# Latent mixer: order of the state factors, the first two heads' scores, the pooling products and the pooled splits

## The reference, cut to what matters

```python
h_lat, h_ctx = mlstm_bidir(p[..., :M_COLS], pc[..., :M_COLS], conv_w[l], conv_b[l], w_q[l], w_k[l], i_bias[l], f_bias[l])
mix = jnp.concatenate([mlstm_out(h_lat, p[..., 2 * M_W:3 * M_W], head_norm[l]),
                       pool_mixer(p[..., M_COLS:], pool_w[l], pool_scale[l], True)], axis=-1)
x = ada_out(x, mix @ w_out[l], mod, 1, norm_post[l, 1], 1.0)
```

## Time and profile before

| | us |
|---|---|
| median of 3 executions | 2033.75 |
| lowest, highest | 2031.55, 2034.03 |
| the profiled execution, its own time | 2034.56 |
| its span, first to last instruction | 2032.7 |
| TensorE busy (matmul) | 1994.2 |
| VectorE busy | 1351.2 |
| ScalarE busy | 1104.4 |
| mean granted TensorE clock | 0.997 |

### The profile page before, as it was taken

One profiled execution on the slowest core, in us unless ns is written; L12 is line 12 of the kernel. 1 busy time (PEld: TensorE's weight loads), 2 busy tenths in 40 slices (PEclk: granted clock), 3 DMA queues, 4 the chain that ended last, 5 costly groups with the idle time before them and its releaser, 6 DMA issues.

```text
span 2032.7 us, 27622 instructions
## 1 busy us (share of the span) xinstructions
PE 1994.2 (98%) x10892; PEld 1687.8 (83%) x10892; DVE 1351.2 (66%) x2199; ACT 1104.4 (54%) x1722; POOL 74.1 (4%) x151
## 2 busy tenths in 40 slices
PE   7999999999989999999999999999999999999998
PEld 5988899987768888888897788888888897788887
DVE  4457676666777556655598897655665587987652
ACT  4344466445565446554646766545654646666552
POOL 0000000001010000000100000000000100000000
PEclk9999999999999999999999999999999999999999
DMA  9797755674257746655533466555755534457551
GB/s 340 250 305 257 236 189 178 208 266 156 99 187 246 229 157 217 205 180 206 198 125 127 145 227 218 184 170 160 239 179 197 204 120 149 142 190 235 186 184 45
DMA packets 281906, 392.91 MB, mean 193 GB/s; under 512 B 9612, under 2 KB 175932, under 8 KB 281648
## 3 DMA queue, kind: packets, MB, share of 16 engines
q1 hardware_dynamic: 277616, 379.62, 56.8%
q0 software_dynamic: 3184, 9.02, 1.3%
q10 hardware_dynamic: 976, 2.49, 0.3%
HBM read 390.04 MB, written 1.05 MB: 192 GB/s over the span
## 4 chain that ended last, share of the span: by engine, by line
PE 83%; DVE 6%; issue 4%; ACT 3%; DMA 2%; POOL 1%; SPq 0%; DVEq 0%; POOLq 0%; ACTq 0%
PE bank L946 20%; PE bank L948 20%; PE bank L947 20%; PE bank L910 20%; DMA raw<-in_ffn_w_in 2%; DVE wlo L2133 1%; PE bank L1086 1%; DVE junk L2832 1%; ACT whi L1533 1%; PE bank L994 1%; DVE wlo L2138 1%; ACT whi L1538 0%; DVE tm L2989 0%; ACT full L1604 0%; ACT junk L1593 0%
## 5 line engine op out<-in xcount | busy, mean ns | idle before, releaser
L2133 DVE TENSOR_TENSOR wlo<-raw,whi 128x1024 fp32r<-128x1024 f32 x360 | 435.0, 1224 | 272.3 <-ACT whi L1533 270.2
L1533 ACT ACTIVATE whi<-raw 128x1024 fp32r<-128x1024 f32 x360 | 376.3, 1058 | 381.4 <-PE bank L948 223.6
L946 PE MATMUL bank<-whi,xTh 128*128 128x512 f32 (+1 forms) x1344 | 528.7, 393 | 6.0 <-issue 3.6
L948 PE MATMUL bank<-whi,xTl 128*128 128x512 f32 (+1 forms) x1344 | 520.7, 387 | 0.0
L947 PE MATMUL bank<-wlo,xTh 128*128 128x512 f32 (+1 forms) x1344 | 520.0, 387 | 0.0
L2138 DVE SCALAR_TENSOR_TENSOR wlo<-raw,cols,whi 128x512 fp32r<-128x512 f32 (+2 forms) x608 | 407.1, 722 | 149.9 <-ACT whi L1538 146.6
L1538 ACT ACTIVATE whi<-raw,cols 128x512 fp32r<-128x512 f32 (+2 forms) x608 | 385.6, 696 | 147.0 <-PE bank L948 110.1
L946 PEld LDWEIGHTS bank<-whi,xTh 128*128 128x128 f32 x1344 | 252.6, 188 | 59.7 <-issue 7.2
L948 PEld LDWEIGHTS bank<-whi,xTl 128*128 128x128 f32 x1344 | 252.4, 188 | 52.3
L947 PEld LDWEIGHTS bank<-wlo,xTh 128*128 128x128 f32 x1344 | 252.8, 188 | 49.0 <-issue 0.5
L910 PE MATMUL bank<-xTh,whi 128*128 128x256 f32 x696 | 197.9, 284 | 0.0
(11 more groups left out here) (375 smaller groups left out, 2447.6 us busy)
## 6 DMA issues: line engine op xcount, KB each, us to landing
raw<-in_w_in SPq DMA_DIRECT2D x68, 1024.0 KB, 5.2
raw<-in_ffn_w_in SPq DMA_DIRECT2D x132, 512.0 KB, 5.8
raw<-in_ffn_w_gate SPq DMA_DIRECT2D x88, 512.0 KB, 4.1
raw<-in_ffn_w_up SPq DMA_DIRECT2D x88, 512.0 KB, 5.1
raw<-in_ffn_w_down SPq DMA_DIRECT2D x40, 1024.0 KB, 5.0
raw<-in_w_mod SPq DMA_DIRECT2D x36, 1024.0 KB, 5.6
raw<-in_ffn_w_out SPq DMA_DIRECT2D x30, 1024.0 KB, 5.7
raw<-in_w_out SPq DMA_DIRECT2D x12, 1024.0 KB, 5.1
```

What stands on the lines that cost most here:

```text
L946: e.matmul(o, hi[:, kc, sl], wh[:, c], start=at == 0 and k == 0, stop=False)
L948: ins = e.matmul(o, lo[:, kc, sl], wh[:, c], start=False, stop=fin)
L1533: e.activation(wh, raw, ACT.Copy).then_inc(m.whi_done, 1)
L2133: e.tensor_tensor(wl, raw, wh.bitcast(F32), ALU.subtract).then_inc(m.wlo_done, 1)
```

## The change

On TensorE, AO's matmuls come ahead of the means (and of the wait for pm), and the pooling products come behind E 0 and E 1, ahead of E 2. The banks are dealt in the same order. On ScalarE, the high half of the first pooled pair is made behind the exponential of head 4, and of the second behind that of head 5. On VectorE, only two of the four weight splits are made ahead of Cx, and the other two behind the eight S; the scaling of the pooled rows goes from ahead of the loop to behind head 1 in it; the low halves of the pooled rows are made behind the division of heads 3 and 4 (k = 5 and 6). No instruction is added or removed.

```diff
@@ Tables.latent
         self.take("TO", "x")
+        self.take("AO")
         for n in range(2):
             self.take("mean", n)
-        self.take("AO")
         for d in DIRECTIONS:
             for p in range(2):
                 self.take("st", d, 2, p)
-        for n in range(2):
-            self.take("pool", n)
         for k in range(10):
+            if k == 2:
+                for n in range(2):
+                    self.take("pool", n)
@@ Tensor.latent
+        bank, full = self.bank("AO")
+        e.wait_ge(m.st_exp, 1)
+        for j in range(8):
+            ins = self.mm(bank[:, 4 * j:4 * j + 3], m.selj[:, j, :], m.mst[:, 9:12], j == 0, j == 7)
+        ins.then_inc(full, 1)
         e.wait_ge(m.ld_pm, 16)
         for n in range(2):
             bank, full = self.bank("mean", n)
...
-        bank, full = self.bank("AO")
-        e.wait_ge(m.st_exp, 1)
-        for j in range(8):
-            ins = self.mm(bank[:, 4 * j:4 * j + 3], m.selj[:, j, :], m.mst[:, 9:12], j == 0, j == 7)
-        ins.then_inc(full, 1)
         for d in DIRECTIONS:
             self.evacuated("kt", d)
             self.states(d, 2, m.kt[:, d, :], m.kv, 16 + 4 * d)
-        for n in range(2):
-            self.evacuated("mean", n)
-            bank, full = self.bank("pool", n)
-            for g in (2 * n, 2 * n + 1):
-                ins = self.mm(bank[:, g % 2 * 256:g % 2 * 256 + 256], m.wp[:, g, :], m.dT[:, g, :], g % 2 == 0, g % 2 == 1)
-            ins.then_inc(full, 1)
         e.wait_ge(m.mlm_done, 1)
         for k in range(10):
+            if k == 2:
+                self.pools()
             if k < 8:
@@ Scalar.latent, in the loop over k and behind it
-        for n in range(2):
-            self.evacuated("pool", n)
-            self.hi(m.xTh[:, 4 + 2 * n:6 + 2 * n, :].rearrange("p c n -> p (c n)"), m.yT[:, n, :])
+            if k in (4, 5):
+                self.evacuated("pool", k - 4)
+                self.hi(m.xTh[:, 2 * k - 4:2 * k - 2, :].rearrange("p c n -> p (c n)"), m.yT[:, k - 4, :])
@@ Vector.latent
-        self.force(self.used + 4)
+        self.force(self.used + 2)
         bank, free = self.filled("TO", "x")
...
         first = [self.step() for _ in range(8)]
-        for n in range(2):
-            bank, free = self.filled("pool", n)
-            for g in range(2):
-                s = CV["ps"] + 2 * n + g
-                ins = e.tensor_scalar(m.yT[:, n, g * 256:g * 256 + 256], bank[:, g * 256:g * 256 + 256], m.cols[:, s:s + 1], None, ALU.mult)
-            ins.then_inc(free, 1)
+        self.force(self.used + 4)
         for k in range(10):
...
+            if k == 1:
+                self.pooled()
             if k >= 2:
                 self.attended(k - 2)
-        for n in range(2):
-            o = [t[:, 4 + 2 * n:6 + 2 * n, :].rearrange("p c n -> p (c n)") for t in (m.xTl, m.xTh)]
-            self.lo(o[0], m.yT[:, n, :], o[1]).then_inc(m.mt_done, 1)
+            if k in (5, 6):
+                o = [t[:, 2 * k - 6:2 * k - 4, :].rearrange("p c n -> p (c n)") for t in (m.xTl, m.xTh)]
+                self.lo(o[0], m.yT[:, k - 5, :], o[1]).then_inc(m.mt_done, 1)
```

More of the change, by code:

```diff
@@ L1293, in latent, with pools @@
         self.mod()
+    def pools(self):
+        m = self.m
+        for n in range(2):
+            self.evacuated("mean", n)
+            bank, full = self.bank("pool", n)
+            for g in (2 * n, 2 * n + 1):
+                ins = self.mm(bank[:, g % 2 * 256:g % 2 * 256 + 256], m.wp[:, g, :], m.dT[:, g, :], g % 2 == 0, g % 2 == 1)
+            ins.then_inc(full, 1)
     def values(self, k):
@@ L2747, in latent, with pooled @@
         self.settle()
+    def pooled(self):
+        m, e = self.m, self.e
+        for n in range(2):
+            bank, free = self.filled("pool", n)
+            for g in range(2):
+                s = CV["ps"] + 2 * n + g
+                ins = e.tensor_scalar(m.yT[:, n, g * 256:g * 256 + 256], bank[:, g * 256:g * 256 + 256], m.cols[:, s:s + 1], None, ALU.mult)
+            ins.then_inc(free, 1)
     def latent_gates(self):
```

## The result

| | before | changed |
|---|---|---|
| median of 20 executions, us | 2032.80 | 2040.28 |
| lowest, highest | 2031.55, 2035.36 | 2031.05, 2043.22 |
| profiled execution, its own time (span) | 2034.56 (2032.7) | 2040.67 (2038.9) |
| its mean granted TensorE clock | 0.997 | 0.993 |

The changed kernel takes 1.0032 of the time of before, 95% interval 1.0026 to 1.0038: slower by 6.5 us by this ratio and by 7.5 in the medians, where 0.9 faster was forecast. (The forecast of 2032.8 started from a median of three executions, 2033.75. That it equals the median of before over 20 executions is chance; what is compared is the difference.) The 20 executions fall in two groups.

A forecast was written before the change was run, and what follows sets the result against it. TensorE, busy 98% of the span, was taken as the bound, leaving its idle time and slow stretches. At the second gate 1.35 gained less 0.41 lost gives 0.94 us, from 2033.75 to 2032.8; range 2030.4 to 2035.3.

The forecast's parts named there:

- the second gate at the fifth part: At the fifth w_out weight part, 9 us behind the first gate: TensorE waits there for VectorE's low halves of the gated heads.
- Rival (b): The gate at the fifth w_out part is not real, so the full 2.89 us is gained: 2030.9; chance 0.1.
- Part 1: TensorE order: AO ahead of the means, E0 and E1 ahead of the pooling products; third score product starts 1.42 us earlier.
- the two early waits: TensorE's 0.79 us for the pooling matrix before the means and 0.63 us for scaled values before the state products both go.
- Part 2: VectorE's work meanwhile: loop over the heads starts at 543.4, not 545.57; second output product gains 1.35 us.
- Rival (a): Low clock comes in the means instead of the pooling products, costing 1.25 us: 2034.1; chance 0.2.
- The Trainium skill's rule on transposes: Transposes don't count as clock activity as matmuls do; by it the clock falls sooner, in the means, giving 2034.1.
- the wait of 1.54 us: TensorE's wait before the first product with w_out, for VectorE's pooled low halves; forecast to go.
- the known one of about 0.94 us: TensorE's wait before the second head's output product, 0.94 us in the kernel before.
- Part 3: Pooled splits beside the heads: low halves push VectorE by 0.205 us each, 0.41 us lost in the last heads.

The follow-up runs named there:

- e3: Kernel before with one edit: high and low halves of the pooled rows made beside the heads; median 2034.34 beside 2034.31, ratio 1.0004.
- e7: Kernel of e1 with the low halves of the pooled rows back behind the loop; median 2029.6, ratio 0.9977 to the kernel before.
- e8: Kernel before with one edit: AO ahead of the wait for the pooling matrix and of the means; median 2031.83 beside 2033.6, ratio 0.9989.
- e1: Changed kernel, but VectorE makes the S of heads 2 and 3 ahead of scaling the pooled rows; median 2029.65, ratio 0.998 to the kernel before.
- e5: Changed kernel with eight extra dense TensorE passes, results unused, behind the output product of k = 4; median 2036.6, ratio 1.0013 to the kernel before.
- e4: Changed kernel with eight extra dense TensorE passes, results unused, in the wait ahead of E 3; median 2032.25, ratio 0.9992 to the kernel before.
- e11: Kernel of e7 once more, on another chip, beside a repeat of e1; median 2029.04, ratio 0.9973 to the kernel before.
- e9: Changed kernel, but only the first pooled pair is scaled behind head 1, the second behind head 3's S; median 2039.69 us.
- e2: Kernel before with one edit: VectorE scales the pooled rows behind head 1; median 2043.13, ratio 1.0048.
- e6: Changed kernel, but S of head 2 alone goes ahead of scaling the pooled rows; median 2040.77, ratio 1.0037 to the kernel before.

## Why the prediction was wrong, point by point

**What bounds the kernel.** Right: the second gate at the fifth part is real (e3), and the low halves behind the loop were hidden by the square of the heads (e7). Rival (b) falls.

**Part 1.** Right in kind: the two early waits go, and e8 gives 1.8 us for it. Mis-sized in two terms: I carried the pooling products at the 3.08 us of the earlier trace rows and the state products at 2.27 into the new order. Both prices held a part at half clock. After, they took 544.44 - 542.62 = 1.82 and 1.88.

**Part 2.** This is where it failed. VectorE's side was right in its order and nearly in its size: from the transposes of TO to the loop it is 542.73 - 531.50 = 11.23 us in e1, where the means ran at the full clock and 543.4 - 531.71 = 11.69 was forecast. In the changed kernel's profile it is 543.52 - 530.60 = 12.92, which is 1.7 us more by the slow means. TensorE's side was not right: "The banks in the new order ask for nothing that is late" left out that E 3 takes the bank that the S of head 2 frees. By the forecast's own figures this bank came just in time: E 3 would be there at 545.98 + 2.26 = 548.24, and that S ends at 548.2. But with state and pooling products at the full clock TensorE is there 1.3 us before VectorE, which scales pooled rows ahead of that S. The same wait stands in e5 (546.66 us, 1.35), where the means weren't slow. In the profile the second output product still starts 550.40 - 530.60 = 19.80 us behind the transposes and not 20.32 as before: by the plain sum of waits the change was still ahead by 0.5 us at this point.

**The clock.** Rival (a) came true in the profiled execution and in that of e4: 5.41 us for the means in the place of 3.72. The price was 5.25 us start to start for 3.55 in e1, 1.70 more and not 1.25. The Trainium skill's rule on transposes (TensorE: Matmul & The Clock Gate, Part 4: PE-mode transpose) fits these two, but in eight of the ten profiles with AO behind the transposes (e1 and e5 to e11) the means ran at the full clock, and no run separates the transposes from AO's passes. e8 shows that the order pays in its median.

What I missed is the other place: the sum of waits inside a thin loop. And I priced a fall as 1.25 us, by the one in the trace, without asking what work stands behind it. In the kernel before it ended during the dense pooling products, about 3.4 us after it began, and in the slow means after 3.4 us too; in the loop it lasted 20.5 us. The sum of the stage, after less before: 0.52 us ahead at the second output product, then 2.01 - 1.09 = 0.92 more to E 4, 19.35 - 10.83 = 8.52 more to the late projection, and 12.90 - 12.13 = 0.77 less from there to the fifth part, where the wait of 1.54 us is gone. That is 8.15 us, which is the 53.29 - 45.14 of the stages; the medians are 7.5 apart. The Trainium skill (TensorE: Matmul & The Clock Gate, Why this matters for your kernels) warns of long idle gaps between bursts of matmuls; here the longest piece was 1.34 us, and pieces added up (e9).

**The step that failed**, in one sentence: the prediction took the loop over the heads to stay at the full clock and a wait in it to cost its own length, and left only the known one of about 0.94 us there; the runs showed waits of 1.34 + 0.85 us, a clock at half for 20 us behind them, and some 9.4 us (0.92 + 8.52) for it.

**Part 3.** Right as far as the runs can tell: e3 is at 1.0004 (0.9995 to 1.0013), and the stage of e1 is 0.5 us longer than that of e7, where a loss of 0.41 was worked out.

**What stays open.** Why 2 of 20 executions of the changed kernel keep the clock, and 4 of 11 of e9: nothing in the programs differs between them. That the low clock in the means costs time in the end wasn't isolated. What ends the low clock without dense passes isn't either: in all four slow loops with a profile (the changed kernel, e2, e6, e9) it came back some 20.5 us after its fall, each time among the output products behind E 7, so the time passed and the products there can't be told apart.

## What to carry to other kernels

Before a wait is moved or swapped, follow for each product who frees its bank, and add up TensorE's idle time in the stretch, not only the wait that ends last: two waits of about a us in a loop of thin products cost some 9 us here, through the clock. (Thin stands here for the loop's E and output products, dense for products of 128 x 256 back to back.) Where the trace has a stretch at the low clock, the prices in it don't hold in another place. Price a new one by its whole length, which here went with the work behind it: 3.4 us where dense products came (before, and the slow means), some 7 us with dense passes put in (e5), 20.5 us in the loop. On the engine that feeds TensorE, first make what frees banks, then what only has to be done some time: the same instructions in that order (e1) turned 1.0032 into 0.998.

## What the runs showed of the hardware

TensorE's clock, once at 1.2 GHz, stayed there for 20 us in which TensorE counted as busy all the time (20.00 of 20.00 us in e2's window). It came back during eight passes of 128 x 256 put into that stretch (e5), and with the same passes in the place of the first wait it didn't fall (e4). The same loop ran at either clock, depending on how it was entered. Per head, the low clock cost nearly the full factor of two: 4.24 for 2.26 us.
